# Queries and branch B's keys turned in 32x32 blocks by VectorE and carried between partition quarters by DMA, instead of transposed by TensorE

## The reference

```python
a_q, a_kv, i_q, i_k, i_w, b_qkv, c_q, c_kv, c_g, m_g = jnp.split(h @ w_in[l], cuts, axis=-1)
y_a = _dsa_attention(_rope(a_q), _rope(a_k), a_v, _rope(i_q), _rope(i_k), i_w) @ w_branch_a[l]
y_b = _moba_attention(_rope(b_q), _rope(b_k), b_v) @ w_branch_b[l]
y_c = _nsa_attention(c_q, _rope(c_q), k_cmp, v_cmp, _rope(k_slc), v_slc, _rope(k_win), v_win, c_gates) @ w_branch_c[l]
x = x + (g[:, :, 0] * y_a + g[:, :, 1] * y_b + g[:, :, 2] * y_c) @ w_out[l]
```

## Time and profile before

| What | Value |
|---|---|
| median of 3 runs | 1163.5 us (1162.96 to 1163.73) |
| profiled execution | 1163.91 us |
| its span in the profile | 1162.2 us |
| granted PE clock, mean | 0.998 of full speed |
| busy: PE, DVE, ACT | 1153.9, 951.5, 581.7 us |
| HBM read | 209.28 MB, 181 GB/s over the span |

### The profile page before, as it was taken

One profiled execution on the slowest core, in us unless ns is written; L12 is line 12 of the kernel. 1 busy time (PEld: TensorE's weight loads), 2 busy tenths in 40 slices (PEclk: granted clock), 3 DMA queues, 4 the chain that ended last, 5 costly groups with the idle time before them and its releaser, 6 DMA issues.

```text
span 1162.2 us, 16328 instructions
## 1 busy us (share of the span) xinstructions
PE 1153.9 (99%) x5573; PEld 945.9 (81%) x5573; DVE 951.5 (82%) x1788; ACT 581.7 (50%) x757; POOL 31.9 (3%) x67
## 2 busy tenths in 40 slices
PE   9999999999999999999999999999999999999997
PEld 7888888887778888888888888888877788888886
DVE  6877788899977687778887887878999696888777
ACT  6444345447764464344454444454578635434433
POOL 2000000001000000000000000000010000000000
PEclk9999999999999999999999999999999999999999
DMA  8566554765425555655556556556653335655561
GB/s 285 190 214 216 181 188 163 234 203 163 137 80 182 181 157 204 217 191 185 195 177 202 180 173 215 182 189 191 198 180 110 141 135 184 219 181 169 202 234 38
DMA packets 148996, 211.04 MB, mean 182 GB/s; under 512 B 8160, under 2 KB 109136, under 8 KB 148944
## 3 DMA queue, kind: packets, MB, share of 16 engines
q1 hardware_dynamic: 148256, 209.64, 54.5%
q10 hardware_dynamic: 688, 0.71, 0.2%
HBM read 209.28 MB, written 1.05 MB: 181 GB/s over the span
## 4 chain that ended last, share of the span: by engine, by line
PE 99%; DVE 0%; issue 0%; ACT 0%; POOLq 0%; POOL 0%; DVEq 0%
PE ps L1371 30%; PE ps L1373 30%; PE ps L1372 30%; PE ps L1585 2%; PE ps L1421 1%; PE ps L1641 1%; PE ps L1613 1%; PE ps L1390 1%; PE ps L1546 1%; PE ps L1558 0%; PE ps L1765 0%; PE ps L1672 0%; PE ps L1632 0%; DVE x L1000 0%; PE ps L1573 0%
## 5 line engine op out<-in xcount | busy, mean ns | idle before, releaser
L1114 ACT ACTIVATE whi<-raw 128x2048 fp32r<-128x2048 f32 (+1 forms) x195 | 365.9, 1879 | 253.3 <-PE ps L1373 252.2
L536 DVE TENSOR_TENSOR wlo<-raw,whi 128x2048 fp32r<-128x2048 f32 (+1 forms) x195 | 433.9, 2244 | 65.6 <-ACT whi L1114 45.7
L1371 PE MATMUL ps<-whi,ht_hi 128*128 128x512 f32 (+1 forms) x1192 | 465.6, 391 | 0.2
L1373 PE MATMUL ps<-whi,ht_lo 128*128 128x512 f32 (+1 forms) x1192 | 460.8, 387 | 0.0
L1372 PE MATMUL ps<-wlo,ht_hi 128*128 128x512 f32 (+1 forms) x1192 | 460.3, 386 | 0.0
L1373 PEld LDWEIGHTS ps<-whi,ht_lo 128*128 128x128 f32 x1192 | 223.9, 188 | 45.9
L1371 PEld LDWEIGHTS ps<-whi,ht_hi 128*128 128x128 f32 x1192 | 224.0, 188 | 45.0 <-issue 1.4
L1372 PEld LDWEIGHTS ps<-wlo,ht_hi 128*128 128x128 f32 x1192 | 224.1, 188 | 43.9
L598 DVE STREAM_TRANSPOSE scr<-scr 32x128 f32<-32x128 f32 x688 | 208.3, 303 | 10.3
L1371 PE MATMUL ps<-whi,at_hi 128*128 128x512 f32 x304 | 118.5, 390 | 0.0
L1372 PE MATMUL ps<-wlo,at_hi 128*128 128x512 f32 x304 | 118.3, 389 | 0.0
(11 more groups left out here) (176 smaller groups left out, 757.3 us busy)
## 6 DMA issues: line engine op xcount, KB each, us to landing
raw<-in_ffn_w_down_dram SPq DMA_DIRECT2D x88, 512.0 KB, 4.9
raw<-in_w_in_dram SPq DMA_DIRECT2D x88, 512.0 KB, 4.5
raw<-in_ffn_w_gate_dram SPq DMA_DIRECT2D x85, 512.0 KB, 4.0
raw<-in_ffn_w_up_dram SPq DMA_DIRECT2D x85, 512.0 KB, 5.0
raw<-in_w_out_dram SPq DMA_DIRECT2D x16, 512.0 KB, 4.4
raw<-in_w_branch_c_dram SPq DMA_DIRECT2D x8, 512.0 KB, 4.4
raw<-in_w_branch_b_dram SPq DMA_DIRECT2D x4, 512.0 KB, 3.9
raw<-in_w_branch_a_dram SPq DMA_DIRECT2D x4, 512.0 KB, 4.0
```

Source lines behind the costliest of these rows:

```text
L536: nc.vector.tensor_tensor(wlo[:, n, 0:w], raw[:, n, 0:w], whi[:, n, 0:w].bitcast(F32), ALU.subtract).then_inc(lo_done, 1)
L1114: nc.scalar.activation(whi[:, n, 0:w], raw[:, n, 0:w], ACT.Copy).then_inc(hi_done, 1)
L1371: nc.tensor.matmul(o, xh, wh, start=start, stop=False)
L1373: return nc.tensor.matmul(o, xl, wh, start=False, stop=stop)
```

## The change

- The fills of queries are gone. FILLS keeps the three pair fills (keys of A and the index, and the two sets of branch C), and the two compression fills follow: five fills with 10 transposes. T1 is 1: one pair fill stands between slabs 12 and 13, the other four between 13 and 14. `by_act` then gives three of them to ACT and two (one pair fill, one compression fill) to DVE.
- `rope` writes into three places instead of `rs`: `rs_1` (queries of A, I and B, keys of B: 8 blocks of 128), `rs_2` (rotated queries of C: 4 blocks) and `pairs`.
- DVE turns `rs_1` after slab 8 with two transposes of 128 partitions by 1024 columns, and `rs_2` together with the raw queries in `pr` after slab 11 with eight of 128 by 256. Each 32x32 block is turned in place, so the result still lies in the wrong quarter of the partitions.
- SP carries the quarters: 16 DMAs for each of the two sets, each from 32 partitions to 32 partitions, 2 KB a partition. They are issued behind loads 11 to 14 (four each) and 15 to 17 (six, five, five), each parcel behind a wait for DVE's turns.
- The results `qk_1` and `qk_2` hold for each partition 128 columns x 8 blocks x 2 halves of the sequence. `scores` reads them in place, so neighbouring columns of an operand are 16 numbers apart. That holds for all queries, for branch B's keys and for the raw queries of C.
- New waits: SP waits for all 16 transfers of the first set before it loads `w1[0][1]`, now ahead of load 15; DVE waits for them before it clears `cmpm` (moved from the mixer's start to behind slab 14); PE waits for the first set before the scores of I and for the second before those of C.
- The factor 1/8 moves from the fills to the operations that follow the scores. The gates' layout in `gr` changes; the `gate` view's blocks are ordered by branch first.

```diff
-FILLS = [((0, 1), "qs", 0), ((2,), "pair", 0), ((6, 7), "qs", 4),
-         ((14,), "pair", 4), ((15,), "pair", 6), ((10, 11), "qs", 6), ((12, 13), "qs", 8),
-         ((16, 17), "n", 0), ((18, 19), "n", 2)]
+FILLS = [((0,), 0), ((1,), 2), ((2,), 4)]
 NFILL = len(FILLS) + 2
-T1 = 3
-
-DVE_TURNS = {"I": (3, "q", 2), "K": (8, "k", 2)}
+T1 = 1
+
+
+CROSS = {11: (0, 0, 4), 12: (0, 4, 8), 13: (0, 8, 12), 14: (0, 12, 16), 15: (1, 0, 6), 16: (1, 6, 11), 17: (1, 11, 16)}
...
+        qk_2 = gr[:, 4096:6144].rearrange("p (c b t) -> p c b t", b=NTURN, t=NT)
+        qk_1 = sb("qk_1", [P, SEQ // NT, NTURN, NT])
+        turned_x = sb("turned_x", [P, 1024])
...
+        def queries(row, b, t):
+
+            return qk_1[row, :, b, t] if b < NTURN else qk_2[row, :, b - NTURN, t]
+
+        def keys(row, pair, kb, j, nt):
+
+            if pair == "B":
+                return qk_1[row, :, BKEYS + j, 0:nt].rearrange("p c t -> p t c")
+            return k_t[row, kb, 0:nt * P]
...
+            def turn_blocks(l, n):
+
                 own(l)
-                for a in range(*rows, 32):
-                    for q in range(0, P, 32):
-                        step(nc.vector.transpose(into[q:q + 32, :, :, a:a + 32], rs[a:a + 32, :, b:b + 2, q:q + 32]))
+                for t in range(NT):
+                    parts = [(0, rs_1[:, t])] if n == 0 else [(0, rs_2[:, t]), (4, pr[:, t, C_Q:C_Q + 512].rearrange(
+                        "p (b c) -> p b c", b=4))]
+                    for b0, src in parts:
+                        nb = src.shape[1]
+                        for q0, into in [(0, turned_1)] if n == 0 else [(0, turned_2[0]), (2, turned_2[1])]:
+                            nq = into.shape[1]
+                            dst = into.rearrange("p q (c b t) -> p q b t c", b=NTURN, t=NT)
+                            step(nc.vector.transpose(dst[:, :, b0:b0 + nb, t, :],
+                                                     src.rearrange("p b (q c) -> p q b c", q=4)[:, q0:q0 + nq]), ("turn", n))
...
-                step(nc.vector.memset(cmpm[:, :, :, :], 0.0), ("cmpm zero",))
...
-                    if m == 7:
-                        turn_blocks(l, "K", (0, 64))
-                    if m == 9:
-                        turn_blocks(l, "K", (64, P))
+                    if m == 8:
+                        turn_blocks(l, 0)
                     if m == 10:
                         rope(l, 3)
                     if m == 11:
-                        turn_blocks(l, "I")
+                        turn_blocks(l, 1)
...
                 rope(l, 5)
                 convert(l, S + 14)
+                dve.wait_ge(crossed[0], (l + 1) * 256)
+                step(nc.vector.memset(cmpm[:, :, :, :], 0.0), ("cmpm zero",))
...
+                if e < 2:
+                    pe.wait_ge(crossed[e], (l + 1) * 256)
...
-                    ins = nc.tensor.matmul(score_head(t, h), q_t[row, qb + h // 2, t * P:(t + 1) * P],
-                                           k_t[row, kb + kstep * (h // 2), 0:nk], start=opens, stop=n >= 6,
+                    ins = nc.tensor.matmul(score_head(t, h), queries(row, qb + h // 2, t),
+                                           keys(row, pair, kb, h // 2, t + 1), start=opens, stop=n >= 6,
...
-                wait_step(pe, l, ("rope", 3))
+                wait_step(pe, l, ("rope", 1))
...
+            def cross(l, m):
+
+                if m not in CROSS:
+                    return
+                n, k0, k1 = CROSS[m]
+                wait_step(sp, l, ("turn", n))
+                for k in range(k0, k1):
+                    a, q = k // 4, k % 4
+                    rows_in_q, rows_in_a = slice(32 * q, 32 * q + 32), slice(32 * a, 32 * a + 32)
+                    dst = (qk_1, qk_2)[n][rows_in_q, 32 * a:32 * a + 32, :, :].rearrange("p c b t -> p (c b t)")
+                    sp.dma_start(dst, turned_blocks(n, q)[rows_in_a]).then_inc(crossed[n], 16)
...
-                for m in (13, 14):
-                    load_halves(l, S + m, w_in, 512 * (m - 13), 4, M_G, 512)
-                for q in range(2, 12):
-                    if q == 5:
-
-                        sp.wait_ge(fill_ps, (l + 1) * NFILL)
+                    cross(l, m)
+                for q in range(12):
+                    if q == 2:
+                        sp.wait_ge(crossed[0], (l + 1) * 256)
                         sp.dma_start(w1[0][1], rows_cols(cmp_w1_k, l, 8 * P, 8, 0, P)).then_inc(w1_in[0], 16)
                     load_halves(l, S + 13 + q, w_in, 512 * (q % 2), 4, M_G + 512 * (q // 2), 512)
+                    cross(l, 13 + q)
```

More of the change, by code:

```diff
@@ L65 @@
 M_B, M_A, M_C = 25, 26, 27
-QBLK = {"A": 0, "I": 2, "B": 4, "R": 6}
-KBLK = {"A": 0, "I": 1, "B": 2, "S": 4, "W": 6}
-NQB, NKB, NRB = 10, 8, 16
+QBLK = {"A": 0, "I": 2, "B": 4}
+KBLK = {"A": 0, "I": 1, "S": 2, "W": 4}
+BKEYS, NTURN, NKB, NPAIR = 6, 8, 6, 3
 ROPE = {
[L74 to L79, removed]
-}
-FILLS = [((0, 1), "qs", 0), ((2,), "pair", 0), ((6, 7), "qs", 4),
-         ((14,), "pair", 4), ((15,), "pair", 6), ((10, 11), "qs", 6), ((12, 13), "qs", 8),
-         ((16, 17), "n", 0), ((18, 19), "n", 2)]
+    0: [(A_Q, 4, ("first", 0)), (A_K, 1, ("pair", 0, 0))],
+    1: [(I_Q, 4, ("first", 2)), (I_K, 1, ("pair", 0, 1)), (B_Q, 4, ("first", 4))],
+    2: [(B_K, 4, ("first", BKEYS))],
+    3: [(C_Q, 8, ("second", 0))],
+    4: [(C_KS, 2, ("pair", 1))],
+    5: [(C_KW, 2, ("pair", 2))],
+}
+FILLS = [((0,), 0), ((1,), 2), ((2,), 4)]
 NFILL = len(FILLS) + 2
-T1 = 3
-DVE_TURNS = {"I": (3, "q", 2), "K": (8, "k", 2)}
+T1 = 1
+CROSS = {11: (0, 0, 4), 12: (0, 4, 8), 13: (0, 8, 12), 14: (0, 12, 16), 15: (1, 0, 6), 16: (1, 6, 11), 17: (1, 11, 16)}
 def by_act(f):
@@ L127 @@
 LAST_ORDER = [0, 2, 1, 3]
-V_STEPS = 277
+V_STEPS = 249
 SETUP_WARM, SETUP_G = 1, 19
@@ L180, in build, with turned_blocks @@
         sc_t = w1_k[:, SEQ:2 * SEQ]
-        qn_t = prob[:, 1, 512:1536].rearrange("p (b c) -> p b c", b=4)
+        turned_2 = [v.rearrange("p (q c) -> p q c", q=2) for v in (prob_all[:, 2048:3072], turned_x[:, :])]
+        def turned_blocks(n, q):
+            return turned_1[:, q, :] if n == 0 else turned_2[q // 2][:, q % 2, :]
         cos_s = sb("cos_s", [P, NT, HD])
@@ L273, in build @@
         fill_a = sem("fill_a")
+        crossed = [sem(f"crossed{n}") for n in range(2)]
         v_step = sem("v_step")
@@ L474, in copy_fill @@
                 return
[L475 to L482, removed]
+            b = FILLS[f][1]
+            for g in range(2):
+                for half in range(2):
+                    copy(k_t[half * HD:(half + 1) * HD, b + g, :], ps[g * HD:(g + 1) * HD, bank, 0:SEQ], 1.0)
         def load_x(eng, n):
@@ L660, in rope @@
                 dve.wait_ge(proj_done, l * 12 + 2 * u + 2)
-                for c0, nh, b0, part in ROPE[u]:
+                for c0, nh, place in ROPE[u]:
                     src = pr[:, :, c0:c0 + nh * HD].rearrange("p t (h c) -> p t h c", h=nh)
+                    into, b0 = {"first": rs_1, "second": rs_2, "pair": pairs}[place[0]], place[1]
                     if nh == 1:
-                        dst = rs[:, :, b0:b0 + 1, part * HD:part * HD + HD]
+                        dst = into[:, :, b0:b0 + 1, place[2] * HD:place[2] * HD + HD]
                     else:
-                        dst = rs[:, :, b0:b0 + nh // 2, :].rearrange("p t b (e c) -> p t (b e) c", e=2)
+                        dst = into[:, :, b0:b0 + nh // 2, :].rearrange("p t b (e c) -> p t (b e) c", e=2)
                     tmp = rtmp[:, :, 0:nh, :]
@@ L750, in maxima @@
                         for h in range(4):
-                            step(nc.vector.tensor_tensor_reduce(prob_view(b, t)[:, h, :], score_head(t, h), mk, -1.0,
+                            step(nc.vector.tensor_tensor_reduce(prob_view(b, t)[:, h, :], score_head(t, h), mk, -ATT_SCALE,
                                                                 -TAKEN, ALU.add, ALU.min,
@@ L1315, in mixer @@
                         eng.wait_ge(cscores_ps, l + 1)
-                        nc.scalar.activation(sc_t, ps[:, 4, 0:SEQ], ACT.Copy).then_inc(cscores_out, 1)
+                        nc.scalar.activation(sc_t, ps[:, 4, 0:SEQ], ACT.Copy, scale=ATT_SCALE).then_inc(cscores_out, 1)
                     if e > 0:
@@ L1539, in fill @@
                         if f < len(FILLS):
-                            b = FILLS[f][0][j]
-                            src = rs[:, t, b, :] if b < NRB else \
-                                pr[:, t, C_Q + (b - NRB) * P:C_Q + (b - NRB + 1) * P]
+                            src = pairs[:, t, FILLS[f][0][j], :]
                         else:
@@ L1568, in scores @@
                     wait_step(pe, l, ("max", e - 1, 1))
-                qb, kb, kstep, _, _ = heads_of(pair) if pair != "C" else (0,) * 5
+                if e < 2:
+                    pe.wait_ge(crossed[e], (l + 1) * 256)
+                qb, kb, _ = heads_of(pair) if pair != "C" else (0,) * 3
                 if pair == "C":
@@ L1633, in weighted @@
```

(4 more changed lines are left out.)

27 lines of the change are left out of this document (13 added, 14 removed).

## The result

The changed kernel takes 1174.49 us (median of 4 runs, 1173.54 to 1175.3) against 1163.53 for the kernel before: ratio 1.0095, 95% interval 1.0077 to 1.0112. Run again later, five times, it took 1173.57 (1173.37 to 1173.8), ratio 1.0087 (1.0073 to 1.0101). The forecast was 1161.9, about no change, in a range of 1160.3 to 1172.5; the result lies above it.

A forecast was written before the change was run, and what follows sets the result against it. PE's own work was taken to bound the kernel. From the median of 1163.5 us, -2.5 for removed transposes and +0.9 for branch C's strided streams, -1.6 in all, gave 1161.9 us, range 1160.3 to 1172.5.

The forecast's parts named there:

- What bounds the kernel: Whole kernel: PE's own work is the time; a microsecond taken from PE counts once, unless PE then waits for something beside it.
- First fill group, gain 0: Ahead of slab 13: 8 of ten transposes (0.89 us) removed, but PE still waits for DVE's rest of slab 13.
- Second group, -1.77: Between slabs 13 and 14: 16 of 24 transposes a layer removed, 1.77 us; net gain 1.25 a layer, 2.5 in all.
- the DVE chain: DVE from slab 14's rest through moved memset, gates, fills and windows ends at 264.1; PE, ready at 263.6, waits 0.5 us.
- For one stream I take zero: Score matmuls reading operands 64 B apart, one stream at a time: no extra PE cost, 0 us.
- rival 1: Strided reads cost PE in score calls, branch B's keys and branch C: 1169.7 to 1174.8 us, likeliest 1171; chance 0.36.
- the main case: The forecast's own sum, 1161.9 us, with bounds 1160.4 to 1165; chance 0.52.
- Branch C, +0.45 a layer: Branch C's four simultaneous strided streams: +0.45 us a layer, 0.9 in all, between zero and serial streams at +1.9.
- Rival 2: Both fill groups: the whole 5.3 us of removed transposes is gained, 1158.2 us; chance 0.06.
- DVE's turns, 1.24 and 0.43 us: DVE's new transposes of 128x1024 and 128x256: 1.24 and 0.43 us each, 5.9 a layer for 9.7, nothing on the path.
- SP, at zero: SP's transfers between slab loads: parcels of 1.8 to 2.7 us, hidden behind 5 us of cover, cost zero.
- Rival 3: SP is late: small transfers delay slab 14 or 15 by 2.7 us a layer, 1167 us; chance 0.06.

The follow-up runs named there:

- Experiment 1: Changed kernel with all score-matmul operands read from adjacent columns (wrong values), turns and transfers kept: 1160.93 us, ratio 0.9978.
- experiments 7 and 8: 7: experiment 6's first form, memset cut to pad columns, 1160.58 us. 8: that plus reordered fills and ACT copying slab 14 ahead of its fills, 1159.34 us.
- experiment 6: Changed kernel, turned data laid out anew: first form step two, runs of 256 B, 1161.41 us; second form adjacent columns, runs of 128 B, 1161.42 us.
- Experiment 9: Experiments 7 and 8's edits on experiment 6's second form: 1162.17 us; experiment 6's first form with each carrying transfer split in two: 1182.52 us.

## Why the prediction was wrong

- **What bounds the kernel** (PE, each microsecond counts once unless something beside it is late): held. Experiment 1 gained what PE gained, and experiments 7 and 8 gained where PE waited.
- **First fill group, gain 0**: held. PE waits 0.97 us for the rest of slab 13.
- **Second group, -1.77, and the DVE chain, which takes 0.5 of it**: held. Slab 14 comes 1.9 us earlier, PE waits 0.56 us for the windows, the compression comes 1.25 us earlier, as forecast. Both layers: 2.5 against 2.5, and 2.6 by experiment 1's time.
- **"For one stream I take zero": the step that failed.** I argued from columns a nanosecond, that the 64-row streams pass half of what PE shows elsewhere, so that half of the port was free. But no column rate of a dense read says what a read at a step costs. The runs show a load of 304 ns instead of 186 and +0.75 us a call for queries alone; the streamed keys add 0.61 in branch B's call. The term that was zero measured 5.9 us a layer, 11.7 in all. The nearest row that showed a read at such a step was DVE's windows in the earlier trace rows, 1.7 ns a column. It was the better guide, but too low: it gives 0.22 us for each of a call's eight steps, and 2.26 / 8 = 0.28 us were measured, 2.2 ns a column. I had it as the lever of rival 1 and gave the main case to a row of the right engine and the wrong pattern.
- **Branch C, +0.45 a layer**: 0.52 measured. Four streams at once only doubled (0.57 to 1.09), so the far bound, serial streams at 1.9, was far off.
- **Rival 2** (all of the 5.3 us gained) did not happen: PE waits 0.97 us for slab 13 and 0.56 for the windows.
- **Rival 1** (chance 0.36) is what happened, at 1169.7 to 1174.8, likeliest 1171. It was low by 2.6 us against the second set of runs: its +0.43 a call was +0.75, and it counted six calls and branch B's in them, where each layer has six and branch B's besides (224 loads over two layers, 16 in a call, are 14 calls). The upper end of the range, 1172.5, had cut off the upper quarter of this very rival, and the result lay there. The chances were nearer than the number: slower had 0.40, the most of the three outcomes, and the number followed the main case's 0.52.
- **DVE's turns, 1.24 and 0.43 us**: 1.97 and 0.60 measured, the first between my two bounds, the second at the upper one; 1.22 and 0.40 once they write at 8 B (experiment 6). The estimate was right for the work and had left out that the writes step by 64 B. Hidden in any case, as forecast.
- **SP, at zero**: right for this kernel, with less room than I had. Four transfers take 2.4 us of SP and six 3.7, against 1.8 to 2.7 forecast, since each takes 0.6 us instead of the 0.44 taken from a load's issue; the second set is out at 264.6, not 262. One reading behind the zero was wrong: loads 15 on were to wait for DVE's slab 12 anyway. DVE had its rest done at 247.1, and SP stood waiting for the first set to land until 249.99, two such waits in all:

```profile
SPq L1894 <- DMA qk<-gates: 8.9, 2, 4.8
```

So load 15 went out at 250.40 instead of 247.69, and the six issues behind it made load 16 later still, 255.26 instead of 251.43. ACT's copy of slab 16 already waited 1.40 us for its data, still beside PE's work. Experiment 9 shows where that ends.

- **Rival 3** (SP late) did not happen here, and did in experiment 9.

## What to carry to other kernels

Ask of every operand of 4-byte elements that PE loads or streams whether two neighbouring elements share 16 bytes: if they don't, price it from a row with the same step (one of DVE came within a quarter of PE's price here), and never from the rate of dense reads. Where a layout has to be interleaved, let the innermost pair be adjacent; it was all but free for PE, made DVE's writes faster, and with runs of 256 B the transfers stayed hidden. Transfers put into a queue of loads, and a wait for their landing ahead of the next load, use up cover that no busy share shows; read the next load's issue time, and expect a later improvement elsewhere to lay it bare.

## What I had not expected of the hardware

- Loads by step are not monotone: 2.38 us at 4 elements, 2.29 at 6, 2.65 at 12, 2.26 at 16. Why 12 is the worst was not taken apart.
- DVE's block transpose pays for where it writes: 128x1024 in 1974 ns with writes 64 B apart, 1222 with 8 B.
- A small transfer from SBUF to SBUF costs SP more to issue than a load of 512 KB (0.44 in the earlier trace rows), and halving its bytes doesn't make it cheaper. The view of one line gives the median and the longest issue: 0.59 and 1.55 us with runs of 2 KB, 0.61 and 1.83 with 256 B, 0.63 to 0.79 (by source buffer) and 3.54 with 128 B, 0.60 and 1.92 for transfers of half the size. The long ones are few, and it is they that make load 16 late. What SP waits for in them the trace doesn't name.
- A long wait costs PE more than the wait. Behind waits of 2.27 to 7.10 us its matmuls started 0.43 us apart instead of 0.23 for some time (granted clock 0.55 from 275 to 281 us), which cost 1.6 to 2.5 us more for each wait (experiment 9).
